# Opening of a two-block transformer kernel: input in four transfers on two queues, turns interleaved with the first matmuls, panels 0 and 1 in pieces

## The reference, cut to what matters

```python
def rms_norm(x, w):
    var = jnp.mean(xf * xf, axis=-1, keepdims=True)
    return (xf * lax.rsqrt(var + EPS) * w).astype(x.dtype)
...
    xn = rms_norm(x, norm1_w[l])
    z = xn @ w_in[l]
    (q, k_c, v_c, k_s, v_s, k_w, v_w, g_nsa, xr, gr, g_a, g_b) = jnp.split(z, IN_SPLITS, axis=-1)
```

## Time and profile before

| | us |
|---|---|
| three runs, median (lowest to highest) | 953.19 (953.05 to 953.20) |
| the profiled execution, its own device time | 953.28 |
| its span | 951.4 |
| PE busy of the span | 943.7 |
| PE's idle time ahead of matmuls that the trace puts down to a wait: on the memset at the start | 1.2 |
| the same, on DVE's low part of panel 4 | 0.2 |

### The profile page before, as it was taken

The page is one execution under the profiler, slowest core; times in us unless marked ns, Lnnn a source line. Parts: engine busy times, 40 slices in busy tenths (PEclk is TensorE's granted clock), DMA queues, the critical chain, the costliest instruction groups (busy, mean ns, idle before and its releaser), DMA issues.

```text
span 951.4 us, 13952 instructions
## 1 busy us (share of the span) xinstructions
PE 943.7 (99%) x5400; PEld 826.8 (87%) x5400; DVE 666.1 (70%) x857; ACT 535.9 (56%) x691; POOL 61.4 (6%) x95
## 2 busy tenths in 40 slices
PE   9999999999999999999999999999999999999997
PEld 8999988888888888898888888999888898888886
DVE  7888869876655565688666666878887586665665
ACT  7687688535444444474454445679674465444544
POOL 1200000002000000022221000100100020000000
PEclk9999999999999999999999999999999999999999
DMA  9784335553855655557766655545435555755541
GB/s 300 224 250 157 114 129 179 190 182 118 273 187 189 207 178 181 182 166 237 211 205 201 207 177 177 179 137 172 133 133 177 177 190 187 220 178 183 194 153 44
DMA packets 119471, 173.14 MB, mean 182 GB/s; under 512 B 3168, under 2 KB 91488, under 8 KB 119424
## 3 DMA queue, kind: packets, MB, share of 16 engines
q1 hardware_dynamic: 117904, 168.41, 55.1%
q0 software_dynamic: 1376, 3.81, 1.3%
q10 hardware_dynamic: 144, 0.26, 0.1%
HBM read 171.42 MB, written 1.05 MB: 181 GB/s over the span
## 4 chain that ended last, share of the span: by engine, by line
PE 98%; DVE 1%; DMA 1%; SPq 0%; ACT 0%; issue 0%
PE pair L713 22%; PE pair L716 11%; PE acc L695 10%; PE acc L697 10%; PE acc L696 10%; PE pair L695 8%; PE pair L697 8%; PE pair L696 8%; PE acc L1058 1%; PE pair L924 1%; PE acc L1207 1%; PE acc L840 1%; DMA raw<-in_w_in 1%; PE acc L907 1%; PE acc L1232 1%; PE acc L1222 0%
## 5 line engine op out<-in xcount | busy, mean ns | idle before, releaser
L713 PE MATMUL pair<-actp,wh 128*128 128x512 f32 x912 | 292.8, 396 | 0.0
L1799 DVE TENSOR_TENSOR wl<-raw,wh 128x2048 fp32r<-128x2048 f32 x89 | 204.8, 2302 | 62.7 <-ACT wh L1331 62.6
L1331 ACT ACTIVATE wh<-raw 128x2048 fp32r<-128x2048 f32 x88 | 168.3, 1913 | 84.1 <-PE acc L697 84.1
L716 PEld LDWEIGHTS pair<-actp,wl 128*128 128x128 f32 x912 | 171.3, 188 | 39.9
L716 PE MATMUL pair<-actp,wl 128*128 128x256 f32 x912 | 179.2, 278 | 0.0
L1795 DVE TENSOR_TENSOR wl<-raw,wh 128x2048 fp32r<-128x2048 f32 x68 | 155.6, 2290 | 32.2 <-ACT wh L1325 31.6
L1325 ACT ACTIVATE wh<-raw 128x2048 fp32r<-128x2048 f32 x69 | 132.1, 1916 | 72.3 <-PE pair L697 43.9
L713 PEld LDWEIGHTS pair<-actp,wh 128*128 128x128 f32 x912 | 141.6, 189 | 1.4
L1546 ACT ACTIVATE arena<-pair 128x512 f32<-128x512 f32 x57 | 34.1, 598 | 170.7 <-PE pair L713 170.7
L695 PE MATMUL acc<-wh,midh 128*128 128x512 f32 x310 | 120.9, 390 | 0.0
L697 PE MATMUL acc<-wh,midl 128*128 128x512 f32 x310 | 120.6, 389 | 0.0
(11 more groups left out here) (363 smaller groups left out, 1391.7 us busy)
## 6 DMA issues: line engine op xcount, KB each, us to landing
raw<-in_w_in SPq DMA_DIRECT2D x35, 1024.0 KB, 5.3
raw<-in_mlp_w SPq DMA_DIRECT2D x32, 1024.0 KB, 5.2
raw<-in_ffn_w_gate SPq DMA_DIRECT2D x22, 1024.0 KB, 5.4
raw<-in_ffn_w_up SPq DMA_DIRECT2D x22, 1024.0 KB, 5.4
raw<-in_ffn_w_down SPq DMA_DIRECT2D x22, 1024.0 KB, 4.9
raw<-in_w_out SPq DMA_DIRECT2D x8, 1024.0 KB, 4.9
raw<-in_w_up_rnn SPq DMA_DIRECT2D x4, 1024.0 KB, 5.0
raw<-in_w_in SPq DMA_DIRECT2D x5, 512.0 KB, 5.9
```

Source lines behind the costliest of these rows:

```text
L713: return nc.tensor.matmul(bank[:, :].rearrange("p (u t) -> p u t", u=2), h[:, k, cs], actp[:, :, k, :], **kw)
L716: return nc.tensor.matmul(bank[:, 0:T], l[:, k, cs], acth[:, k, :], **kw)
L1331: nc.scalar.activation(wh[:, slot(n), :], raw[:, slot(n), :], ACT.Copy).then_inc(hi_ready, 1)
L1799: nc.vector.tensor_tensor(wl[:, slot(n), :], raw[:, slot(n), :], wh[:, slot(n), :].bitcast(F32), ALU.subtract).then_inc(lo_ready, 1)
```

## The change

1. The input is loaded in four transfers of 256 KB: the left halves by SP (`left_loaded`), the right halves by ACT's own queue (`right_loaded`), issued as ACT's first two instructions.
2. `WARM` is 6 in place of 7.
3. PE turns both left halves first; the 8 transposes of the right halves go, two at a time, behind each k of panel 0's first near sweep.
4. Panel 0's near half is loaded, cast and split in two quarters (k = 0..1 and 2..3); the DVE order is cast, cast, subtract, subtract.
5. ACT writes the high parts of k = 4, 5 before it casts panel 0's far half, and k = 6, 7 behind it.
6. Panel 1 is loaded and cast in two halves (`second_hi`, then `hi_ready`); its first 8 matmuls need only the first.
7. Panel 2 takes panel 1's order (all `wh` matmuls of a column half first), so that its `lo` is needed 16 matmuls later.

```diff
-WARM = 7
+WARM = 6
...
             for tt in range(TT):
-                sp.dma_start(xt[:, tt, :], a["x"][0, tt * P:(tt + 1) * P, :]).then_inc(x_loaded[tt], 16)
+                sp.dma_start(xt[:, tt, 0:512], a["x"][0, tt * P:(tt + 1) * P, 0:512]).then_inc(left_loaded[tt], 16)
...
-            for hf, loaded in enumerate((half_loaded, panel_loaded[0])):
-                ks = slice(KT // 2 * hf, KT // 2 * (hf + 1))
-                sp.dma_start(pv(0, KT, raw)[:, ks, :], up_src(w_in, col1[0])[:, ks, :]).then_inc(loaded, 16)
-            for n in range(1, UPA):
+            for n, k0, k1, loaded in ((0, 0, 2, quarter_loaded[0]), (0, 2, 4, quarter_loaded[1]), (0, 4, KT, panel_loaded[0]),
+                                      (1, 0, 4, second_loaded), (1, 4, KT, panel_loaded[1])):
+                sp.dma_start(pv(n, KT, raw)[:, k0:k1, :], up_src(w_in, col1[n])[:, k0:k1, :]).then_inc(loaded, 16)
+            for n in range(2, UPA):
...
-                pe.wait_ge(half_hi, 1)
-                sweep(near, h, acth, acth_ready)
-                pe.wait_ge(half_lo, 1)
-                sweep(near, l, acth, acth_ready)
+                for k in near:
+                    sweep((k,), h, acth, acth_ready, quarters=quarter_hi)
+                    at = KT // 2 + 2 * (k % 2)
+                    turn_part(0, 1 + k // 2 * 2, (at, at + 1))
+                sweep(near, l, acth, acth_ready, quarters=quarter_lo)
...
-            turn_tokens(0)
+            for b in (0, 2):
+                turn_part(0, b, range(KT // 2))
...
-            second_panel().then_inc(panel_done, 1)
-            for n in range(KCVC, UPA):
+            high_first(1).then_inc(panel_done, 1)
+            free_bank(KCVC)
+            high_first(KCVC).then_inc(panel_done, 1)
+            for n in range(KSKW, UPA):
...
+            for tt in range(TT):
+                act.dma_start(xt[:, tt, 512:D], a["x"][0, tt * P:(tt + 1) * P, 512:D]).then_inc(right_loaded[tt], 16)
             act.wait_ge(mhalf_set, 1)
...
             norm_hi(0, V_N1, range(KT // 2))
+            norm_hi(0, V_N1, range(KT // 2, KT - 2))
             act.wait_ge(panel_loaded[0], 16)
             nc.scalar.activation(wh[:, slot(0), PW // 2:PW], raw[:, slot(0), PW // 2:PW], ACT.Copy).then_inc(hi_ready, 1)
-            norm_hi(0, V_N1, range(KT // 2, KT))
-            hi(1)
+            norm_hi(0, V_N1, range(KT - 2, KT))
+            for loaded, cs, ready in ((second_loaded, slice(0, PW // 2), second_hi), (panel_loaded[1], slice(PW // 2, PW), hi_ready)):
+                act.wait_ge(loaded, 16)
+                nc.scalar.activation(wh[:, slot(1), cs], raw[:, slot(1), cs], ACT.Copy).then_inc(ready, 1)
...
-            dve.wait_ge(half_loaded, 16)
-            nc.vector.tensor_copy(wh[:, slot(0), 0:PW // 2], raw[:, slot(0), 0:PW // 2]).then_inc(half_hi, 1)
-            dve.wait_ge(half_hi, 1)
-            nc.vector.tensor_tensor(wl[:, slot(0), 0:PW // 2], raw[:, slot(0), 0:PW // 2], wh[:, slot(0), 0:PW // 2].bitcast(F32),
-                                    ALU.subtract).then_inc(half_lo, 1)
+            for i in range(2):
+                cs = slice(PW // 4 * i, PW // 4 * (i + 1))
+                dve.wait_ge(quarter_loaded[i], 16)
+                nc.vector.tensor_copy(wh[:, slot(0), cs], raw[:, slot(0), cs]).then_inc(quarter_hi, 1)
+            for i in range(2):
+                cs = slice(PW // 4 * i, PW // 4 * (i + 1))
+                dve.wait_ge(quarter_hi, i + 1)
+                nc.vector.tensor_tensor(wl[:, slot(0), cs], raw[:, slot(0), cs], wh[:, slot(0), cs].bitcast(F32),
+                                        ALU.subtract).then_inc(quarter_lo, 1)
```

More of the change, by code:

```diff
@@ L230, in norm_col @@
             return fw[:, k:k + 1] if j == 2 else vcol(v, k)
-        x_loaded = [sem(f"x_loaded{tt}") for tt in range(TT)]
+        left_loaded = [sem(f"left_loaded{tt}") for tt in range(TT)]
+        right_loaded = [sem(f"right_loaded{tt}") for tt in range(TT)]
         id_loaded = sem("id_loaded")
@@ L248, in build @@
         piece_loaded = [sem(f"piece_loaded{s}") for s in range(2)]
-        half_loaded = sem("half_loaded")
-        half_hi = sem("half_hi")
-        half_lo = sem("half_lo")
+        quarter_loaded = [sem(f"quarter_loaded{i}") for i in range(2)]
+        quarter_hi = sem("quarter_hi")
+        quarter_lo = sem("quarter_lo")
+        second_loaded = sem("second_loaded")
+        second_hi = sem("second_hi")
         hi_ready = sem("hi_ready")
@@ L762, in turn_part @@
                         m.then_inc(xs_turned, 1)
-            def turn_tokens(j):
-                for b in range(2 * TT):
-                    turn_part(j, b, range(4 * (b % 2), 4 * (b % 2) + 4))
             def first_panel(n, outs, j):
@@ L834, in opening_panel, with sweep @@
                 h, l = pv(0, KT, wh), pv(0, KT, wl)
-                def sweep(ks, w, x, ready, stop=False):
+                def sweep(ks, w, x, ready, stop=False, quarters=None):
                     for k in ks:
+                        if quarters is not None:
+                            pe.wait_ge(quarters, k // 2 + 1)
                         pe.wait_ge(ready, k + 1)
@@ L854, in opening_panel, with high_first @@
                 return sweep(far, h, actl, actl_ready, True)
-            def second_panel():
-                h, l = pv(1, KT, wh), pv(1, KT, wl)
-                pe.wait_ge(hi_ready, 2)
+            def high_first(n):
+                h, l = pv(n, KT, wh), pv(n, KT, wl)
+                if n == 1:
+                    pe.wait_ge(second_hi, 1)
+                else:
+                    pe.wait_ge(hi_ready, n + 1)
                 for c in range(2):
-                    cs, out_ = slice(c * P, (c + 1) * P), ps[1][:, c * T:(c + 1) * T]
+                    cs, out_ = slice(c * P, (c + 1) * P), ps[n % 2][:, c * T:(c + 1) * T]
                     for k in range(KT):
+                        if c == 0 and k == KT // 2:
+                            pe.wait_ge(hi_ready, n + 1)
                         nc.tensor.matmul(out_, h[:, k, cs], acth[:, k, :], start=k == 0, stop=False)
                         nc.tensor.matmul(out_, h[:, k, cs], actl[:, k, :], start=False, stop=False)
-                    split(1)
+                    split(n)
                     for k in range(KT):
@@ L1371, in _ @@
             for tt in range(TT):
-                act.wait_ge(x_loaded[tt], 16)
+                act.wait_ge(left_loaded[tt], 16)
                 nc.scalar.activation(xs[:, tt, 0:512], xt[:, tt, 0:512], ACT.Square, scale=ROOT,
@@ L1790, in lo @@
             def lo(n):
+                if n == 1:
+                    dve.wait_ge(second_hi, 1)
                 dve.wait_ge(hi_ready, n + 1)
@@ L1831, in _ @@
             for tt in range(TT):
-                dve.wait_ge(x_loaded[tt], 16)
+                dve.wait_ge(right_loaded[tt], 16)
                 right = xt[:, tt, 512:D]
```

## The result

| | before | changed |
|---|---|---|
| median of 21 runs, us | 953.27 | 954.42 |
| lowest to highest | 952.93 to 954.20 | 953.86 to 955.83 |
| profiled execution, its own time | 953.28 | 954.72 |
| its span | 951.4 | 952.5 |

The changed kernel is slower: ratio 1.0013, 95% interval 1.0007 to 1.0019, 1.15 us. That is within the 0.2% to which the forecast gave 0.92, but above its range of 952.3 to 953.7, and of the other sign than its 0.2 us gained. The 21 runs form two groups: 14 of 953.86 to 954.97 (median 954.14) and 7 of 955.11 to 955.83 (median 955.46), with a mean granted clock of 0.996 or 0.997 in the second and 0.998 to 1.000 in the first. Only 0.14 us lies between the groups, so it is the clock that tells them apart. In what follows they are the early and the late group. None of the 21 runs of before was like the second.

The account below looks back on a forecast made before the run. PE was taken as the bound, busy 943.7 of 951.4 us, so only its opening could gain. Panel 1's `wl` matmuls 0.2 us earlier gave span 951.2; with time outside the span, 953.0 us, range 952.3 to 953.7.

Parts of the forecast that it names:

- PE's first near sweep: Panel 0: first matmul at 8.5, moved transposes mostly fill PE's waits for ACT, second near sweep at 10.15 instead of 10.49.
- ACT's order: ACT's far cast of panel 0 ends 0.8 us later, at 11.85, but DVE meets it level, without a wait.
- Input: Opening token load: four pieces on two queues land 0.1 us earlier than the two whole tiles.
- The ramp that the forecast hoped for: Opening token load: a second queue could carry 370 instead of 287 GB/s in the 2nd microsecond, gaining 0.2 us.
- rule on batches: Input transfers: batches of at least 1 MiB; four pieces taken one behind the other would be some 4 us later.
- DVE's gain of 0.23: Panel 0's near half in quarters: DVE's subtractions end at 10.20 instead of 10.43.
- The place that decides: Panel 1's low part on DVE: ends at 17.07 instead of 17.24, so PE's `wl` matmuls gain 0.2 us.
- Panel 2 and on: After panel 1: high-first order gains nothing, the 0.2 us passes on, and the gap at 33.14 stays.
- The time around the span: Outside the span: the profiled execution's own time stays 1.88 us over its span.
- The slow clock: Opening: PE loses its full rate in gaps from 6.2 to 8.5; 2.3 us lost, 955.5; chance 0.05.
- 5.0 us of unbroken work: Opening zero matmuls: PE's full rate shows only after this much uninterrupted work.

Follow-up runs that it names:

- e3: Changed kernel with the input loaded as before, two whole 512 KB transfers from SP alone; median 953.74 us, span 951.6.
- e4: Changed kernel with all 16 transposes ahead of panel 0's near sweep, left halves then right halves; median 953.44 us, span 951.3.
- e2: Changed kernel with WARM = 7 again; median 954.07 us, span 951.9.
- f2: Changed kernel with WARM = 4; median 955.33 us, span 953.2, all 11 runs late.
- g1: Changed kernel unaltered, run again on another chip; median 954.07 us, span 951.9, 2 of 11 runs late.
- h3: Changed kernel with WARM = 5; median 955.17 us, span 953.0, 9 of 11 runs late.
- h4: Changed kernel unaltered, one more profiled execution; 953.90 us in a single run, span 951.7.
- e1: Kernel before with WARM = 6 and nothing else changed; median 953.24 us, span 951.3.
- f1: Kernel before with five more semaphores allocated and unused; median 953.24 us, span 951.3.
- f3: Changed kernel without the second queue and the interleaving, with WARM = 7; quarters, halves, left halves first and ACT's order remain; median 952.97 us, span 950.8.
- f4: Kernel before with only panel 1 loaded and cast in halves and panel 2 high first; median 953.33 us, span 951.2.
- g3: f3 with panel 1 loaded and cast in one piece; median 952.74 us, span 950.7.
- h1: Kernel before with panel 2 loaded in two halves, still cast in one instruction; median 953.12 us, span 951.2.
- h2: g3 again on another chip; median 953.00 us, span 951.0.
- g2: Kernel before with the input in four 256 KB transfers, all from SP; median 953.95 us, span 952.1.
- g4: f3 with the transfers of the identity and the vectors issued by ACT instead of SP; median 953.31 us, span 951.1.

## Why the prediction was wrong

**The interleaved transposes (step "PE's first near sweep").** The failed claim is that about 0.75 of the 1.0 us of moved transposes "fills time in which PE waited for ACT". It rested on the first matmul at 8.5, which needed ACT's first high part at 8.03. But ACT was busy with its own right halves until 7.07 + 1.32 = 8.39 in the changed profile; the high part ran from 8.47, and PE could start 0.14 behind its end of 8.95, at 9.09. That is 0.59 of the 0.74 by which the near `wl` sweep missed its mark (10.89 against 10.15); the rest is a sweep of 1.80 in place of the forecast's 1.65. A late input explains only a part: in e3, with the tokens about as in before, the first matmul still comes at 8.89.

The wait for ACT was there, but ahead of the first matmul, where the moved transposes used to stand. Without them PE stands still for 0.50 us (the row at 9.09), and taking 0.80 us of transposes away (8.54 to 9.34 in e4) brings the first matmul only 0.25 forward, or 0.14 counted from the first transpose. In the sweep they lengthen PE's work from 1.27 to 1.80, by 0.53. By then ACT was ahead of PE: its fourth part ended at 10.04, and PE needed it at 10.44. They also held back ACT's far parts and through them DVE's far low part, which the forecast had seen only as a question of ACT's order.

**The input (step "Input").** Forecast 0.1 earlier. In the seven profiles in which ACT loads the right halves (changed, e2, e4, f2, g1, h3, h4) the last piece of tile 1 landed at 5.87 to 6.30, against 5.69 to 5.84 in the nine in which SP loads whole tiles and ACT nothing (before, e1, e3, f1, f3, f4, g3, h1, h2). DVE started on tile 0 at 4.55 to 4.94 against 4.06 to 4.59. The runs give 0.33 us for taking the queue out (e3). The ramp that the forecast hoped for did not come. In the window from 1 to 2 us the profile of before (first row) moves 57 GB/s (last column), that of the changed kernel 10:

```profile
1.00:2.00 1.00, 0.81 (x2) 0.72 (x3) 0.13 (x1) 1.00 (x1) 1.00 (x1) 1.00 0.36 57
1.00:2.00 1.00, 0.81 (x2) 0.72 (x3) 0.13 (x1) 0.34 (x1) 1.00 (x1) 1.00 0.04 10
```

That pair is the extreme: the same window has 10 to 47 GB/s in the seven and 29 to 74 in the nine, so it points the same way but does not part them.

The Trainium skill ("Trainium Kernel Development and Optimization", section "Key Constraints") says that transfers issued from several engines share the same 16 DMA engines, so that a second issuer saves only the sequencer's issue time. The runs agree: the issues were saved (g2 against the changed kernel), the landing did not come sooner. The Trainium skill's rule on batches that the prediction had weighed ("DMA: Bandwidth & Descriptors", section "Bandwidth"; that page measured it, like the 2 us, on transfers issued by GpSimd, while SP and ACT issue here) has the right sign in g2, though not the 4 us of the estimate: 0.9 us.

**DVE's gain of 0.23** was too small. The casts took 0.42 to 0.43 (0.40 assumed), but the second quarter landed at 8.17 and not at 8.46, and the two subtractions end at 9.82 against 10.20 forecast and 10.43 before: 0.61 gained. It did not decide: in f3, with the two costs taken away, DVE is done at 9.81 and the near `wl` sweep starts at 10.20, behind PE's own sweep. The gain there needs the earlier turns as well (f3 beside h1).

**"The place that decides"** was DVE's low part of panel 1, forecast to end at 17.07. It ended at 17.59, delayed by the transposes through ACT, and PE came later still. In f3 and h2 DVE started sooner than forecast (14.16 and 14.55, not 14.78), and PE arrived just when the forecast said it would, 16.9 and 17.0, and was not held. The forecast was too pessimistic here.

**Panel 2 and on**: right. The gap ahead of panel 4 stayed 0.2, and the rest passed on, apart from the wait of 0.6 us at 57 us in one execution, behind a late transfer. Its place has no slack: in before ACT's copy ended at 56.45 and PE used it at 56.51.

**The time around the span.** The forecast took before's 1.88 as a constant. It averages 1.90 in before and in e1, f1, g2 and h1, and 2.2 in every one with the full change: 0.3 us of the loss. Excluded as cause, each by a run: ACT's queue (e3), semaphores (f1), the number of transfers from SP (g2, g4), one more weight transfer (h1). Present in part where only the halves and the high-first order are in (f4, 2.05) and where panel 1's halves are out (g3, h2, 2.0). What it is stays open.

**The slow clock** was given 0.05 and came in 9 of 32 runs. Its price was right, 955.5 forecast and 955.46 the late group's median, though that includes 0.87 that has other causes: the late runs stand 1.3 over the early ones. Its argument against itself, "the rate had risen by 6.4, and no gap is over 0.6 us", read one profile, and the gap itself grew: 0.70 us ahead of the turns here, 1.77 in g1. In the sixteen profiles with six or seven warm matmuls (all but f2 and h3) the first shortened record starts anywhere from 3.9 (e1, e2) to 6.9 us (f1, f3, g4, h1), so the forecast's 5.0 us of unbroken work was one draw of many. In five of them it starts at 6.47 or later (f4 is the fifth), and six warm matmuls end at 6.6 when none is shortened but the last. The counts go with the dose: in the changed kernel with 7, 6, 5 and 4 warm matmuls 0 of 11, 9 of 32, 9 of 11 and 11 of 11 runs were late. Six are not enough to bring it on alone: e1, e3 and e4 had none in 33 runs, where 28% would give nine. Nor is seven a full guard: one of before's 126 runs was at 956.23 with a mean granted clock of 0.996. What else it takes stays open; e3 and e4 each took away one part (the second queue, the transposes between matmuls), and neither showed a late run, though 0 of 11 has a chance of 0.03 in each at a share of 28%.

In sum: 0.3 outside, 0.6 for the interleaving (e4), 0.3 for the second queue (e3), less the 0.6 gained by the rest (f3's span), make 0.6 to 0.7, where the early runs stand 0.77 (e2) to 0.87 above before; some 0.1 to 0.2 is not accounted for, within what the chips differ by. The late third of the runs lifts the median by another 0.28.

## What to carry to other kernels

Work that is moved between the first matmuls is free only where the matmul engine waits there for longer than that work takes, and the place it leaves must not be one where it stood in a wait already; find out from the other engine's timeline what its first result really waits for, here its own scaling and not the transposes. An earlier landing pays only if nothing else is level with it: the near half of panel 0 was not enough without the earlier turns (h1 beside f3), and each further issue ahead of a transfer can move that transfer's landing (g2). Zero matmuls that warm up TensorE need a margin over the latest step seen in several profiles, and since the late state sits in a part of the runs, one needs more than three of them to see it.

## What the runs showed of the hardware

- Landing follows the issue: in g2 two more issues from SP, of about 0.4 us each, put panel 0's half 0.7 us later although the same bytes were moved.
- The step of PE's record length from 634 to 379 ns, under unbroken matmuls from 1.19 on, began between 3.9 and 6.9 us, in the same program before 5 and at 6.0 (g1, changed kernel). In f2 and h3 it had not come when the zero matmuls ended, and the clock's first entry is at 13.03 and 14.06 us.
- The trace's clock entries begin at that step. A window ahead of the first entry reads 1.00 whatever the rate, so there only the record lengths tell.
- Device time less span lies within 0.15 us in most kernels (around 1.9 or 2.2 us), but within 0.24 to 0.39 in f4, g3 and h2; its mean can change by 0.3 with the program, by something not found here.
- Interleaved with matmuls, two 128 x 128 transposes cost (0.45 - 2 x 0.12) = 0.21 us, about what they cost in a row of their own (0.80 for eight in e4).
